# Pairing the gate and up weights of the narrow experts: 4 KB rows in a ring of six places

## The reference

```python
combine = ...                       # (256, 16): two experts for each token, all in one group of four
for e in range(16):
    he = silu(t @ w_gate[e]) * (t @ w_up[e])      # 256x2048 @ 2048x512, twice
    y = y + combine[:, e:e + 1] * (he @ w_down[e])    # 256x512 @ 512x2048
```

## Time and profile before

| | |
|---|---|
| median of 3 runs | 2733.91 us (2733.82 to 2735.57) |
| profiled execution, its time | 2734.1 us |
| profiled execution, its span | 2732.3 us |
| TensorE (PE) busy | 2626.0 us, 96% of the span |
| VectorE (DVE) busy | 1863.2 us, 68% |
| ScalarE (ACT) busy | 1306.7 us, 48% |
| mean granted TensorE clock | 0.986 |
| moved by DMA | 641.18 MB, mean 235 GB/s |

### The profile page before, as it was taken

How to read it: one execution, slowest core, us unless ns; L and a number is a source line. 1 busy time by engine, 2 the same in 40 slices (tenths; PEclk the granted TensorE clock), 3 DMA queues, 4 the chain that set the end, 5 groups by cost and what they waited for, 6 DMA issues and landing times.

```text
span 2732.3 us, 33657 instructions
## 1 busy us (share of the span) xinstructions
PE 2626.0 (96%) x13173; PEld 2165.6 (79%) x13173; DVE 1863.2 (68%) x2436; ACT 1306.7 (48%) x1697; POOL 102.8 (4%) x104
## 2 busy tenths in 40 slices
PE   4699999999999999999999999999999999999998
PEld 2399888777888888778688688888878888888886
DVE  6988856866777888888877665756554555455445
ACT  2345535455444677777534243444444434443443
POOL 1000000000000000000132310000000000000000
PEclk9899999999999999999999999999999999999999
DMA  9998765617777899999454454554555556655553
GB/s 343 384 372 296 283 242 188 221 51 260 259 266 267 314 369 364 365 361 374 184 199 169 154 192 167 186 184 165 185 190 187 192 190 192 193 185 195 190 191 118
DMA packets 179898, 641.18 MB, mean 235 GB/s; under 512 B 11115, under 2 KB 11196, under 8 KB 137000
## 3 DMA queue, kind: packets, MB, share of 16 engines
q1 hardware_dynamic: 171648, 593.53, 61.3%
q0 software_dynamic: 5264, 27.21, 2.8%
q10 hardware_dynamic: 2840, 18.43, 1.8%
HBM read 632.79 MB, written 6.34 MB: 234 GB/s over the span
## 4 chain that ended last, share of the span: by engine, by line
PE 78%; DVE 8%; DMA 7%; ACT 4%; issue 3%; ACTq 0%; DVEq 0%; SPq 0%
PE ps L2119 76%; DMA raw<-in_stream 4%; DVE w_lo L1222 2%; ACT w_hi L684 2%; DVE raw L1298 2%; DMA under_r<-in_stream 1%; DMA arena<-in_filt_w 1%; DMA arena<-in_stream 1%; PE ps L2282 0%; ACT arena L834 0%; PE ps L2786 0%; ACT arena L705 0%; DVE ps L1442 0%; DVE under_r L1316 0%; DVE arena L2026 0%
## 5 line engine op out<-in xcount | busy, mean ns | idle before, releaser
L1222 DVE TENSOR_TENSOR w_lo<-raw,w_hi 128x1024 fp32r<-128x1024 f32 x968 | 1179.2, 1231 | 674.5 <-ACT w_hi L684 668.1
L684 ACT ACTIVATE w_hi<-raw 128x1024 fp32r<-128x1024 f32 x968 | 1012.1, 1058 | 1028.7 <-PE ps L2119 939.5
L2119 PE MATMUL ps<-w_hi,r_two 128*128 128x512 f32 x3072 | 971.9, 394 | 14.4 <-DVE w_lo L1222 8.5
L2119 PEld LDWEIGHTS ps<-w_hi,r_two 128*128 128x128 f32 x3072 | 578.7, 188 | 145.7 <-DVE w_lo L1222 21.1
L2119 PE MATMUL ps<-w_lo,r_two 128*128 128x512 f32 x1536 | 599.9, 391 | 0.0
L2119 PE MATMUL ps<-h_two,w_hi 128*128 128x256 f32 (+1 forms) x2048 | 556.6, 345 | 3.6 <-DVE w_lo L1222 3.6
L2119 PE MATMUL ps<-w_hi,h_two 128*128 128x512 f32 x1728 | 541.6, 392 | 5.5 <-DVE w_lo L1222 2.9
L2119 PE MATMUL ps<-h_two,w_lo 128*128 128x256 f32 x1536 | 434.1, 283 | 0.0
L2119 PEld LDWEIGHTS ps<-h_two,w_hi 128*128 128x128 f32 x2048 | 355.5, 192 | 52.0 <-issue 6.5
L2119 PEld LDWEIGHTS ps<-w_hi,h_two 128*128 128x128 f32 x1728 | 324.4, 188 | 76.7 <-DVE w_lo L1222 3.9
L2119 PE MATMUL ps<-w_lo,h_two 128*128 128x512 f32 x864 | 336.5, 389 | 0.0
(11 more groups left out here) (344 smaller groups left out, 1445.3 us busy)
## 6 DMA issues: line engine op xcount, KB each, us to landing
raw<-in_stream SPq DMA_DIRECT2D x516, 1024.0 KB, 5.6
under_r<-in_stream SPq DMA_DIRECT2D x58, 512.0 KB, 6.3
arena<-in_mod_units ACTq DMA_DIRECT2D x16, 1024.0 KB, 5.5
arena<-in_stream SPq DMA_DIRECT2D x25, 512.0 KB, 6.4
under_h<-in_stream SPq DMA_DIRECT2D x13, 512.0 KB, 5.7
filters<-arena POOLq DMA_DIRECT2D x4, 1024.0 KB, 8.7
under_r<-filters POOLq DMA_DIRECT2D x4, 1024.0 KB, 6.2
x<-in_x POOLq DMA_DIRECT2D x1, 2048.0 KB, 37.2
```

Source lines behind the costliest of these rows:

```text
L684: act.activation(dst, src, ACT.Copy).then_inc(hi_ready, 1)
L1222: dve.tensor_tensor(low, src, high, ALU.subtract).then_inc(lo_ready, 1)
L2119: return pe.matmul(o, a, b, start=start, stop=stop)
```

## The change

From unit 112 on (`RING_FROM`, the first gate unit of p = 5, the sixth expert) up to unit 231, the weights go round a ring of six places instead of four: the four of `raw` and two more in `arena` at 4096 to 8192. These 120 units are gate and up of p = 5 to 14 and down of p = 4 to 13. A pair of neighbouring gate or up units is moved together, as two transfers of 1 MB with rows of 1024 numbers (4 KB): each transfer brings two of the four pieces for both units of the pair. ScalarE therefore waits for both landings before the first half of a pair. SyncE issues a pair when the place of its second unit is free, so both transfers come behind one wait. Down units stay transfers of 1 MB with 8 KB rows, in the new order of places. The last gate, up and down units (232 to 247) go through four places and in 2 KB rows as before. `diag` moves to another place in `arena`, the landing counts are adapted by `RING_LESS`, and the two loads of GpSimd share a semaphore.

```diff
+RING, RING_FROM, RING_TO = 6, BASE["moe"] + 56, BASE["moe"] + 176
+RING_LESS = (RING_TO - RING_FROM) // SLOTS - (RING_TO - RING_FROM) // RING
+def slot_of(n):
+    return (n - RING_FROM) % RING if in_ring(n) else n % SLOTS
+def landing_of(n):
+    m = n - RING_FROM
+    if in_ring(n):
+        return m // RING + 1 + ((FIRST_UNITS + RING_FROM) // SLOTS if m % RING < SLOTS else 0)
+    return (FIRST_UNITS + n) // SLOTS + 1 - (RING_LESS if n >= RING_TO else 0)
+def split_ahead(n):
+    if not in_ring(n):
+        return 2 * n - 6
+    m = n - RING_FROM
+    return 2 * (n - RING + 2 - m % 2) if m >= RING else 2 * (n - SLOTS + 1) if m < SLOTS else 2 * (BASE["moe"] + 48)
...
-        landed = [sem(f"landed{s}") for s in range(SLOTS)]
+        landed = [sem(f"landed{s}") for s in range(RING)]
-        diag = at(4096, 4, P)
+        diag = at(11008, 4, P)
+        def ring_unit(slot):
+            return raw[:, slot, :] if slot < SLOTS else at(4096 + (slot - SLOTS) * UNIT, UNIT)
+        def ring_pair(slot):
+            return raw[:, slot:slot + 2, :].rearrange("p s n -> p (s n)") if slot < SLOTS else at(4096, 2 * UNIT)
         def halves(n, k, s, whole):
+            if in_ring(n):
+                slot = slot_of(n)
+                if not across(n):
+                    return ring_unit(slot)[:, (k % 2) * HALF:(k % 2 + 1) * HALF], whole
+                eight, c = ring_pair(slot - slot % 2).rearrange("p (j c n) -> p c j n", j=4, c=8), 4 * (slot % 2) + 2 * (k % 2)
+                return eight[:, c:c + 2], whole.rearrange("p (c j n) -> p c j n", c=2, j=4)
...
-                sp.wait_ge(lo_ready, 2 * (BASE["moe"] + n) - 6)
+                unit = BASE["moe"] + n
+                if in_ring(unit) and u < 8:
+                    if u % 2:
+                        continue
+                    sp.wait_ge(lo_ready, split_ahead(unit + 1))
+                    eight = sp_units[bass.ds(first, 8)].rearrange("(j w) p n -> w p j n", w=2)[u // 4][:, :, u % 4 * 512:u % 4 * 512 + 1024]
+                    place = ring_pair(slot_of(unit)).rearrange("p (j n) -> p j n", j=4)
+                    for half in range(2):
+                        sp.dma_start(place[:, 2 * half:2 * half + 2], eight[:, 2 * half:2 * half + 2])\
+                            .then_inc(landed[slot_of(unit) + half], 16)
+                    continue
+                sp.wait_ge(lo_ready, split_ahead(unit))
+                if in_ring(unit):
+                    sp.dma_start(ring_unit(slot_of(unit)), sp_units[bass.ds(first + u, 1)].rearrange("a p n -> (a p) n"))\
+                        .then_inc(landed[slot_of(unit)], 16)
...
+                if k % 2 == 0 and static:
+                    act.wait_ge(landed[slot_of(n)], 16 * landing_of(n))
+                    if in_ring(n) and across(n) and slot_of(n) % 2 == 0:
+                        act.wait_ge(landed[slot_of(n) + 1], 16 * landing_of(n + 1))
```

More of the change, by code:

```diff
@@ L154, in across, with in_ring @@
     return any(0 <= n - BASE[f"ffn_in{part}"] < SIZE[f"ffn_in{part}"] for part in range(3))
+RING, RING_FROM, RING_TO = 6, BASE["moe"] + 56, BASE["moe"] + 176
+RING_LESS = (RING_TO - RING_FROM) // SLOTS - (RING_TO - RING_FROM) // RING
+def in_ring(n):
+    return RING_FROM <= n < RING_TO
+def slot_of(n):
[10 more added lines that the diff above has]
+    return 2 * (n - RING + 2 - m % 2) if m >= RING else 2 * (n - SLOTS + 1) if m < SLOTS else 2 * (BASE["moe"] + 48)
 COLS, NCOLS = {}, 0
@@ L528, in _ @@
                     group.append(sp.value_load(route[0:1, p // 4:p // 4 + 1], min_val=0, max_val=3))
-                sp.wait_ge(lo_ready, 2 * (BASE["moe"] + n) - 6)
+                unit = BASE["moe"] + n
                 first = 48 * group[p // 4] + (ADA_UNITS + BASE["moe"] + 12 * (p % 4))
-                if u < 8:
+                if in_ring(unit) and u < 8:
[12 more added lines that the diff above has]
+                        .then_inc(landed[slot_of(unit)], 16)
+                elif u < 8:
                     quarter = sp_units[bass.ds(first, 8)].rearrange("(j w) p n -> w p j n", w=2)[u // 4][:, :, u % 4 * 512:u % 4 * 512 + 512]
@@ L611, in _ @@
             pool.wait_ge(sem("hidden_t"), N_EXP)
-            load("ld_rowg", (row_x1, d["final_g"].partition_broadcast(P)))
+            load("ld_row", (row_x1, d["final_g"].partition_broadcast(P)))
             def load_filter(b):
@@ L670, in _ @@
             pool.wait_ge(sem("cols_added"), 2 + 8)
-            load("ld_rowf", (row, d["norm_final_g"].partition_broadcast(P)))
+            load("ld_row", (row, d["norm_final_g"].partition_broadcast(P)))
         @block.scalar
         def _(act):
+            fewer = {"landed": 0}
             def hi(g, k):
                 s, static = (k // 2) % SLOTS, isinstance(g, int)
-                if k % 2 == 0:
-                    act.wait_ge(landed[s], 16 * (FIRST_UNITS // SLOTS + 1) + 16 * (g + k // 8))
+                n = 4 * g + k // 2 if static else -1
+                if k % 2 == 0 and static:
+                    act.wait_ge(landed[slot_of(n)], 16 * landing_of(n))
+                    if in_ring(n) and across(n) and slot_of(n) % 2 == 0:
+                        act.wait_ge(landed[slot_of(n) + 1], 16 * landing_of(n + 1))
+                elif k % 2 == 0:
+                    act.wait_ge(landed[s], 16 * (FIRST_UNITS // SLOTS + 1 - fewer["landed"]) + 16 * (g + k // 8))
                 if not (static and 8 * g + k < 4):
                     act.wait_ge(half_done, 8 * g + (k - 3))
-                src, dst = halves(4 * g + k // 2 if static else -1, k, s, w_hi[:, k % 4, :])
+                src, dst = halves(n, k, s, w_hi[:, k % 4, :])
                 act.activation(dst, src, ACT.Copy).then_inc(hi_ready, 1)
@@ L692, in phase @@
             def phase(name, step=None, per_iter=1, unrolled=False):
+                fewer["landed"] = RING_LESS if BASE[name] >= RING_TO else 0
                 def body(g, i, final):
@@ L1818, in add_unsorted @@
                 if cb == 0:
-                    dve.wait_ge(sem("ld_rowg"), 16)
+                    dve.wait_ge(sem("ld_row"), 16)
                 for h in range(TH):
@@ L2072, in last_rows @@
                 if cb == 0:
-                    dve.wait_ge(sem("ld_rowf"), 16)
+                    dve.wait_ge(sem("ld_row"), 32)
                 dve.wait_ge(sem("cols_added"), 2 + 16 + cb + 1)
```

## The result

The changed kernel takes 2719.36 us (median of 5 runs, 2718.23 to 2720.75), the kernel before 2733.91 us in the same comparison (5 runs, 2728.9 to 2735.57). The ratio is 0.9946 with a 95% interval of 0.9932 to 0.996: 14.8 us faster, between 10.9 and 18.6. The forecast was 2726.0, its range ended at 2722.5. A second comparison of the same two kernels (first experiment) gave 0.9966. The profiled execution took 2720.75 us, its span is 2718.9.

What follows compares the result with a forecast made beforehand. Transfers were taken to bound the narrow experts, with TensorE nearly full. The cap of 10.1 us less 2.1 for stalls gave a gain of 8.0, from the median 2733.9 to 2726 us; range 2722.5 to 2731.5.

Steps and rivals of the forecast that it cites:

- the cap: Experts 5 to 15: TensorE's floor of 334.4 us against 344.5 limits any gain from transfers to 10.1 us.
- allowance of 2.1 us for small stalls: Ten narrow experts: 0.2 us each kept for stalls, as transfers (33.1) and TensorE (33.08 or 33.99) are near each other.
- Longer rows: Gate and up units: 4 KB instead of 2 KB rows save 0.17 us each, 13.5 us of transfer time over 80 units.
- rival 1: Narrow experts: transfers stay the bound, rows save only 4.6 us, total about 2730 us; chance 0.20.
- Six places: Weight ring of the narrow experts: two more places count for nothing by themselves, the DMA share being already 1.00.
- Both landings: First half of a pair: waiting for two transfers needs 8.2 us, 9.8 are available, so it costs nothing.
- Rival 2: Ring: the pair wait closes the loop from F = 11.3 us on, costing 20 us, total 2754 us; chance 0.08.
- Way in: Ring's start, pair 112/113 waiting for unit 109: 10.9 us cover the pair's 8.2, so nothing; expert 5 begins full.
- way out: Ring's end, from unit 232 in the small ring: counted as nothing, with 0 to 1.5 us lost or 0.7 gained.
- Nothing behind the experts should give it back: Stages after the experts: if the transposes' distance shrinks but the total doesn't, the prediction is wrong.
- Rival 3: Path from memory: a ceiling in bytes that rows don't move, so no change, 2734 us; chance 0.10.

Runs made afterwards that it cites:

- first experiment: The changed kernel unaltered, run again beside the kernel before: 2722.46 us, ratio 0.9966.
- light kernels: Six single 2 KB places, and the changed kernel, each without the `w_lo` product in the ring's units: 2696.26 and 2709.21 us.
- fillers: The changed kernel with 12 more filler matmuls behind the experts: 2735.37 us, ratio 1.0014 to the kernel before.
- light singles: Single 2 KB transfers in six places, with the `w_lo` product left out in the ring's units: 2696.26 us, one run.
- late loads moved: Single 2 KB transfers in six places, with `LATE_FROM` 7 instead of 12: 2723.85 us, ratio 0.9973 to the kernel before.
- light pairs: The changed kernel (4 KB pairs) with the `w_lo` product left out in the ring's units: 2709.21 us, one run.

## Why the prediction was wrong

The direction and the cap were right. The step that failed is the term for the six places, put at nothing, with the whole gain of the experts given to the rows; and the stages around the experts were put at nothing too. In numbers: the forecast gain was 8.0 us. The ten experts gave 9.5, the stretch in front of them 0.3, the wait at the tail 1.0 and the stages behind 2.6, which is the spans' 13.4; the medians lie 1.1 us further apart (14.55). By the ratio of the second comparison the change would stand at 2724.6, inside the range, so the miss in the total is partly scatter. The miss in the mechanism is not.

*The cap, right.* 33.08 and 33.99 us an expert were predicted as TensorE's floor, 33.13 and 34.04 came; the waits turned from landings to TensorE, as expected. The allowance of 2.1 us for small stalls was mis-sized: 0.5 us remained (334.95 against 334.4). It came from setting transfers at 33.1 an expert, level with TensorE. They were not level: without a third of the matmuls 2 KB singles took 31.4 us an expert and 4 KB pairs 32.1.

*"Longer rows", wrong.* The step took the transfer rate in 2 KB stretches, 344 to 363 GB/s, for a rate of rows. "So the rates carry" rested on one sum that came out at 34.6, but rates read in a kernel give back that kernel's time whatever sets them. The 8 KB rates were also less clear than stated: two more stretches of 8 KB rows (1006 to 1013 and 1075 to 1082) carried 371 and 369 GB/s, below the 374 taken as the low end, and the DMA share in the 8 KB stretches is 0.98, not the 1.00 that rival 1 names. With four places only so much is under way as the loop lets out. The chain of waits in the kernel before, from which the prediction takes nothing, shows it:

```profile
1208.58 1.24 DVE w_lo L1222
...
1209.99 8.56 DMA raw<-in_stream
1218.58 1.07 ACT w_hi L684
...
1219.73 1.08 issue
1220.81 0.74 DVE arena L1804
1221.55 1.14 DVE w_lo L1222
...
1222.86 7.14 DMA raw<-in_stream
1230.02 1.07 ACT w_hi L684
1231.11 2.37 DVE w_lo L1222 x2
...
1233.63 7.95 DMA raw<-in_stream
```

Subtraction ends, SyncE issues, the transfer lands, two halves are rounded and subtracted, and the same place is issued again: 12.87 and 10.77 us for four units, 2.96 on the mean, each through one place. In the whole stretch it is 4 x 2.87 = 11.5: a landing of 7.4, 1.07 of rounding, 2.4 of subtraction, which leaves some 0.6 for VectorE's other work in between. Four places at TensorE's pace allow 11.0, five 13.8, six 16.5, so one place more suffices.

The size of the row's price was not the mistake. Time on the DMA queues for a unit follows from the queue's bytes and share over 280 us (960 to 1240). The lines of the six single places with 2 KB rows and of the change (packets, MB, share):

```profile
q1 hardware_dynamic: 39926, 105.31, 101.7%
```

```profile
q1 hardware_dynamic: 22629, 104.43, 97.4%
```

That is 2.84 and 2.74 us a unit, at the same pace of TensorE: 0.10, or 0.15 for a gate or up unit, near the 0.17 predicted. In the two light kernels it is 2.75 for 2 KB singles and 2.72 for 4 KB pairs, 0.05 for a gate or up unit; the kernel before has 2.90. So rows of 4 KB do shorten the work of the queues, but the time for a unit moves with the kernel around it, and this saving was not what TensorE waited for: with 2.84 us a unit the experts are as fast as with 2.74.

*"Six places", wrong.* "I count nothing for it by itself, since the share is already 1.00." This is the sentence that failed. A share of 1.00 or more stood at 364, 374 and 398 GB/s; it doesn't say that no more bytes could be moved. Five and six places with the old rows gave the whole 9.5 us. The experts' result fell nearly on the cap because either way, by rows or by places, the cap decided.

*"Both landings", right in size, by luck.* The bound F from which a pair closes the ring was put at 11.3 us, against 8.2 in an empty queue and 10.3 to 11.3 in a full one. With 2 KB rows in pairs F reached 10.97 at the place shown, 11.8 at most, and the gain was gone; with 4 KB rows it stayed within 10.4. The luck is that the work beside F, put at 5.9 us, was 7.7 in the round shown, so the true margin was smaller. Rival 2 was a real mechanism, 56 us dear in four places. The Trainium skill ("Perfetto Trace Analysis", DMA Optimizations) has larger transfers (from 2 KB to 4 or 8 KB) as an improvement; no run here shows one that single transfers with 2 KB rows in as many places don't give as well.

*"Way in", "way out", nothing: right.* Expert 5 began full; the tail wait, 2.7 us "in any case", took 1.7, and lies at 1.6 to 2.7 in eight profiles of both kinds.

*"Nothing behind the experts should give it back": right, but nothing was said of what they might give by themselves.* Behind lie 1429.9 to 1436.3 us in twelve profiles (the fillers' 10.3 taken off), and expert 5 stands at 918.3 to 926.5, in values that go neither by the rows nor by the places. The prediction took 0.2% as what can be told, and then drew the range as if medians stood still. The kernel before had medians of 2731.5 to 2733.9 in four comparisons, the change 2719.4 and 2722.5; a range down to 2718 would have allowed for that. What the change itself does is in the experts: 6.4 to 9.5 us (334.95 against 341.36 and 344.48). With the wait at the tail and the 2.6 us behind that makes the two spans' 13.4; whether those 3.6 belong to the changed program or to chance was not shown.

*Rival 3, "no change", wrong.* A ceiling of the path at 374 GB/s doesn't exist: 398 were carried in the same stretch. The limit of about 358 GB/s for a core's transfers from HBM that the Trainium skill gives ("DMA: Bandwidth & Descriptors", Where 436 GB/s comes from) is passed here as well; the same section also mentions a measured 425 GB/s, and the traces, with 398 and 424, go with that.

## What to carry to other kernels

A DMA share of 1.00 is no proof that transfers are at their limit: count the places, take the time from issue to landing, add what must happen before the place is issued again, and divide by the places; if that is above the pace of the consumer, another place is worth more than longer rows. Grouping transfers behind one wait costs places, so it is paid for before it brings anything. And repeat the profile of the kernel before: here the stretch that a loop of waits decides varied by 3 us, the one bound by TensorE by 0.05.

## What the runs showed of the hardware

The second block's stages, behind the experts, change their length with nothing changed in them. In the windows of 1600 to 1700 us, before and after, the granted clock is 0.98 and 0.93:

```profile
1600.00:1700.00 100.00, 100.00 (x552) 84.60 (x551) 63.72 (x83) 45.64 (x65) 0.00 (x0) 0.98 0.47 162
```

```profile
1600.00:1700.00 100.00, 100.00 (x533) 84.31 (x532) 60.69 (x78) 42.58 (x60) 0.00 (x0) 0.93 0.46 162
```

After has one stretch of 13.7 us at the lower level (granted 0.50, 1.2 GHz), from 1633 to 1647 us, with TensorE never idle in front of it; before has three shorter ones, at 1548, 1651 and 1999 us, the first and the last beside idle time of TensorE. In such a stretch two matmuls follow in 0.64 us and behind it in 0.35. The places are not free: after's stretch begins in the same run of small matmuls (128x128 and 1x512) as before's second, and in eleven of the twelve profiles one begins in that run. How long it lasts, and whether the others come, differs between profiles of the same kernel. Besides, the same 800 matmuls of the gate stage take 138.67 us in seven profiles (both of the change, 4 KB pairs in four places, singles in six, fillers, light singles, late loads moved) and 141.34 in five (both of before, pairs of 2 KB, five places, light pairs), at the full clock. The difference is 2.67 us, and 3.5 over all of the some 1070 matmuls that have it; the mean record there was 391 ns after and 399 ns before:

```profile
L2119 PE MATMUL ps<-r_two,w_hi 128*128 128x512 f32 x128 | 45.3, 399 | 0.0
```

```profile
L2185 PE MATMUL ps<-r_two,w_hi 128*128 128x512 f32 x122 | 42.3, 391 | 0.0
```

Both groups hold kernels with four places and with more, with 2 KB and with 4 KB rows, so neither chooses the pace. But the two kernels that were profiled twice kept theirs, so it may belong to the program as built; no run here tells that from chance.

The traces of before and after hold the same 13173 matmul records in the same order, so their starts can be compared one by one. Behind the wait of expert 15, after gains 0.4 us within 50 us, 1.7 and 1.6 where before has its stretches at 1548 and 1999, and 3.5 by the pace; it loses 4.7 by its longer stretch at the lower level. That makes the 2.6 us: a balance of larger terms, of which none was shown to follow from the ring or the rows.
